# One core, hybrid attention and MLP block: first products a pair of tiles sooner, head mix reordered on GpSimd, a weight combination ahead of the token mixes

## What is computed

```python
h = rmsnorm(x, norm_mix)
proj = h @ w_in                                    # heads of two kinds and 8 gates
mixed = concat(swa_attention(...), forgetting_attention(...))
x = x + mixed @ w_out
h = rmsnorm(x, norm_mlp)
u = relu(h @ w_up)
x = x + (u * u) @ w_down
return rmsnorm(x, norm_final)
```

## Time and profile before

| | |
|---|---|
| median of 3 runs | 2398.11 us (2395.19 to 2401.05) |
| the profiled execution | 2394.05 us, its span 2392.4 us |
| TensorE matmul busy | 97% of the span |
| VectorE, ScalarE, GpSimd busy | 64%, 48%, 30% |
| mean granted clock of TensorE | 0.995 |

### The profile page before, as it was taken

One profiled execution on the slowest core, in us unless ns is written; L12 is line 12 of the kernel. 1 busy time (PEld: TensorE's weight loads), 2 busy tenths in 40 slices (PEclk: granted clock), 3 DMA queues, 4 the chain that ended last, 5 costly groups with the idle time before them and its releaser, 6 DMA issues.

```text
span 2392.4 us, 34959 instructions
## 1 busy us (share of the span) xinstructions
PE 2326.6 (97%) x11346; PEld 1934.7 (81%) x11346; DVE 1520.1 (64%) x2623; ACT 1154.1 (48%) x2226; POOL 706.9 (30%) x593
## 2 busy tenths in 40 slices
PE   7999999999999998999899999999999999999998
PEld 5888888788888886887687877888888888888887
DVE  6588873688888886566745655444465555564454
ACT  5211112788888886223545555555553233333243
POOL 2000000111111114235568764666640032120132
PEclk9999999999999999999999999999999999999999
DMA  5567765666666565766455576654457486564464
GB/s 189 215 235 278 268 242 163 180 160 156 160 157 157 152 156 169 248 218 202 170 183 163 189 286 242 202 160 152 154 190 260 165 298 234 193 219 162 138 219 160
DMA packets 253970, 469.09 MB, mean 196 GB/s; under 512 B 59336, under 2 KB 119752, under 8 KB 246032
## 3 DMA queue, kind: packets, MB, share of 16 engines
q1 hardware_dynamic: 247808, 451.11, 58.6%
q0 software_dynamic: 6048, 16.52, 2.6%
HBM read 316.13 MB, written 151.42 MB: 195 GB/s over the span
## 4 chain that ended last, share of the span: by engine, by line
PE 51%; DVE 3%; POOL 2%; issue 2%; DMA 1%; ACT 1%; SPq 0%; POOLq 0%; ACTq 0%; DVEq 0%
PE m_ps L2533 24%; PE m_ps L2556 23%; PE m_ps L1685 4%; DMA b_kept<-f_kept 1%; POOL m_mix L1548 1%; DVE f_up_lo L2389 1%; PE m_ps L2574 0%; DVE m_xn L1653 0%; DVE m_xm L1646 0%; DVE m_mix L1622 0%; ACT m_mix_hi L1585 0%; DVE keep_lo L2408 0%; POOL h_raw L1560 0%; POOL f_kept L2157 0%; DVE hop_lo L1659 0%
## 5 line engine op out<-in xcount | busy, mean ns | idle before, releaser
L2556 PE MATMUL m_ps<-keep_hi,hop_hi 128*128 128x512 f32 x880 | 342.5, 389 | 0.4 <-DVE hop_lo L2392 0.4
L2556 PE MATMUL m_ps<-keep_hi,hop_lo 128*128 128x512 f32 x880 | 342.4, 389 | 0.0
L2556 PE MATMUL m_ps<-keep_lo,hop_hi 128*128 128x512 f32 x880 | 342.3, 389 | 0.0
L2392 DVE TENSOR_TENSOR hop_lo<-h_raw,hop_hi 128x512 fp32r<-128x512 f32 x224 | 176.6, 789 | 236.8 <-ACT hop_hi L2228 236.7
L2389 DVE TENSOR_TENSOR f_up_lo<-wide_raw,f_up_hi 128x512 fp32r<-128x512 f32 x160 | 182.5, 1142 | 223.0 <-ACT f_up_hi L2223 222.9
L2228 ACT ACTIVATE hop_hi<-h_raw 128x512 fp32r<-128x512 f32 x224 | 140.8, 630 | 334.4 <-PE m_ps L2556 330.5
L958 POOL DMA_DIRECT2D o_main<-a_o x63 | 36.5, 580 | 775.2 <-ACT a_o L1326 726.6
L599 PE MATMUL p_ps_o<-p_ht_lo,p_w_hi 128*128 128x512 f32 x576 | 224.5, 390 | 0.0
L2533 PE MATMUL m_ps<-keep_hi,f_up_hi 128*128 128x512 f32 x512 | 202.8, 396 | 6.1 <-DVE f_up_lo L2389 4.7
L2533 PE MATMUL m_ps<-keep_hi,f_up_lo 128*128 128x512 f32 x512 | 201.3, 393 | 0.0
L2533 PE MATMUL m_ps<-keep_lo,f_up_hi 128*128 128x512 f32 x512 | 199.4, 390 | 0.0
(11 more groups left out here) (246 smaller groups left out, 5779.8 us busy)
## 6 DMA issues: line engine op xcount, KB each, us to landing
h_raw<-u_ops SPq DMA_DIRECT2D x224, 256.0 KB, 4.2
wide_raw<-in_w_up SPq DMA_DIRECT2D x32, 1024.0 KB, 7.2
u_ops<-f_u SPq DMA_DIRECT2D x128, 256.0 KB, 4.3
wide_raw<-in_x SPq DMA_DIRECT2D x59, 512.0 KB, 4.0
u_ops<-f_us SPq DMA_DIRECT2D x96, 256.0 KB, 2.3
proj_hi<-p_o_hi SPq DMA_DIRECT2D x17, 1024.0 KB, 6.2
proj_lo<-p_o_lo SPq DMA_DIRECT2D x17, 1024.0 KB, 8.3
h_raw<-in_w_down SPq DMA_DIRECT2D x58, 256.0 KB, 3.9
```

The lines of the kernel that those rows point to most:

```text
L2392: nc.vector.tensor_tensor(lo, a_raw[:, (m - UP) % A_RING], hi.bitcast(F32), ALU.subtract).then_inc(op_lo_done, 1)
L2556: last = nc.tensor.matmul(down_banks[b % 2][t][:], a[:, cols], w[j], start=(j == 0 and m == 0), stop=(j == FG - 1 and m == 2))
```

## The change

Three edits, told here in the order of the program.

**Start.** Product n stands behind the turn of tile 2n + 3 instead of 2n + 5 (the last two products before stood behind all turns; now only product 7 does). ScalarE's squares of tiles 0 to 3 run up to two tiles ahead, from tile 4 on one ahead as before, and their unused output goes to a part of keep_hi that is written last. The two weight splits stand behind tiles 2 and 3 instead of both behind tile 2; VectorE does norm(4) behind the second; product 0 waits for the first weight split alone. The gate columns are transposed behind tile 5 instead of 7.

**Head mix.** The loops are written so that join, divide and split_mix of tile t + 2 stand at the end of step t. On ScalarE, VectorE and TensorE the resulting order of instructions is what it was. On GpSimd join(t + 2) now waits until norm(t) is done, and mix_tokens stands behind it instead of ahead of it.

**MLP.** GpSimd does mix_w(g + 1, 3) ahead of mix_rest instead of behind it; for g = 15 ahead of the wait and of mix_u too.

```diff
-        GATE_TILE = 7
+        GATE_TILE = 5
-        product_after_turn = {t: 2 * (t // TPB - 1) + t % TPB // 2 for t in range(TPB, ST) if t % 2}
+        product_after_turn = {2 * n + TPB - 1: n for n in range(2 * SB - 1)}
@@ scalar
             square(0)
+            square(1)
             for t in range(ST):
-                if t + 1 < ST:
-                    square(t + 1)
+                for ahead in range(t + 1, min(t + 3, ST)):
+                    if ahead == (t + 2 if ahead < X_RING else t + 1):
+                        square(ahead)
                 if t in product_before_turn:
                     split_first(product_before_turn[t])
                 split_ht_hi(t)
-                if t == 2:
-                    split_w_hi(0)
-                    split_w_hi(1)
+                if t in (2, 3):
+                    split_w_hi(t - 2)
@@ vector
-                if t + 1 < ST:
+                if t + 1 < ST and t != 3:
                     norm(t + 1)
...
-                if t == 2:
-                    split_w_lo(0)
-                    split_w_lo(1)
+                if t in (2, 3):
+                    split_w_lo(t - 2)
+                if t == 3:
+                    norm(t + 1)
@@ tensor
-                pe.wait_ge(w_lo_done, 2)
+                pe.wait_ge(w_lo_done, min(n, 1) + 1)
@@ head mix, gpsimd
+            join(1)
             for t in range(ST):
-                if t + 1 < ST:
-                    join(t + 1)
...
                 nc.gpsimd.tensor_tensor(rstd[:, t:t + 1], rstd[:, t:t + 1], mhalf[:], ALU.pow).then_inc(rooted, 1)
+                if t + 2 < ST:
+                    pool.wait_ge(normed, t + 1)
+                    join(t + 2)
                 if KEPT <= t < KEPT + 6:
                     mix_tokens(t - KEPT)
@@ MLP, gpsimd
             if g == FG - 1:
+                mix_w(g + 1, 3)
                 pool.wait_ge(hop_lo_done, hop_count[1, 1])
             if g:
                 mix_u(g - 1)
+            if g + 1 < GROUPS and g != FG - 1:
+                mix_w(g + 1, 3)
             if 2 <= g < 10:
                 mix_rest(*divmod(g - 2, 2))
-            if g + 1 < GROUPS:
-                mix_w(g + 1, 3)
```

More of the change, by code:

```diff
@@ L232, in project @@
         turned_logits = x_in[:, 0, 0:P]
-        squares = whole.raw["p_o_hi0"][:, S - D:S]
+        squares = whole.raw["keep_hi"][:].rearrange("p (k b) s -> p k (b s)", k=DK // 2)[:, :, S - 2 * P:S]
         gate_first = whole.raw["p_o_lo1"][0:G, S - D:S]
@@ L398, in square @@
                     act.wait_ge(squared, t)
-                nc.scalar.activation(squares, x_in[:, t % X_RING], ACT.Square,
+                nc.scalar.activation(squares, x_in[:, t % X_RING].rearrange("p (k c) -> p k c", k=DK // 2), ACT.Square,
                                      accum_out=ssum[:, t:t + 1]).then_inc(squared, 1)
             def split_ht_hi(t):
+                if t == ST - 2:
+                    act.wait_ge(squared, ST)
                 for half in range(2):
@@ L418, in split_first @@
             def split_first(n):
-                if n == 4:
-                    act.wait_ge(squared, ST)
                 split_o_hi(n % 2, n // 2, n % 4, n)
@@ L445, in _ @@
                 split_ht_hi(t)
-                if t == 2:
-                    split_w_hi(0)
-                    split_w_hi(1)
-            for n in range(2 * SB - 3, 2 * SB - 1):
-                split_first(n)
+                if t in (2, 3):
+                    split_w_hi(t - 2)
+            split_first(2 * SB - 2)
             split_w_hi(2)
@@ L625, in _ @@
                     product_first(product_after_turn[t])
-            for n in range(2 * SB - 2, 2 * SB):
-                product_first(n)
+            product_first(2 * SB - 1)
             def scores_first():
@@ L1599, in _ @@
             act.sem_inc(mix_hi_done, 1)
+            split_mix(1)
             for t in range(ST):
-                if t + 1 < ST:
-                    split_mix(t + 1)
-                else:
+                if t == ST - 1:
                     mlp.scalar_first(act)
@@ L1614, in _ @@
                     nc.scalar.activation(hop_hi[:, k], raw[:, 0, k], ACT.Copy).then_inc(hop_hi_done, 1)
+                if t + 2 < ST:
+                    split_mix(t + 2)
             mlp.scalar(act, lambda: copy_ht(ST - 1))
@@ L1632, in _ @@
             dve.sem_inc(mix_lo_done, 1)
+            divide(1)
+            split_mix(1)
             for t in range(ST):
                 slot = t % 2
[L1635 to L1638, removed]
+                if t == ST - 1:
                     mlp.vector_first(dve)
@@ L1660, in _ @@
                                             ALU.subtract).then_inc(hop_lo_done, 1)
+                if t + 2 < ST:
+                    divide(t + 2)
+                    split_mix(t + 2)
             mlp.vector(dve)
```

## The result

The changed kernel takes 2411.1 us (median of 4 runs, 2409.39 to 2412.16) against 2398.07 for the kernel before in the same session, 13.0 us more. The ratio of the timed runs is 1.0059, 95% interval 1.0047 to 1.0071: 0.6% slower. The forecast was a median near 2410, slower, with a range of 2401 to 2416. The profiled execution has a span of 2409.6 us, 17.2 more than the one of before; the granted clock of TensorE falls from 0.995 to 0.992 in the mean.

A forecast was written before the change was run, and what follows sets the result against it. TensorE, busy 97% of the span, was taken as the bound. Start +10.7, head mix +1.6 and MLP -0.2 gave 12.1 us on 2394.05, so 2406.2; with the median 4.1 above that execution, near 2410, range 2401 to 2416.

The forecast's parts named there:

- The stalls: Start: TensorE waits for the just-turned tile's low half, 4.6 us at products 2 and 4, 2.3 at product 6; sum 11.5.
- the chain of 6.07 us: Start of the kernel before: from product 1's end to the odd tile's second low half done, 6.07 us, carried over unchanged.
- The lead: Start: product 0 runs from about 20.4 to 27.7, a lead of 6.0 us, 4.3 left after two tile turns.
- The clock: Start: lower TensorE clock behind the stalls, 1.5 us for each long one, 0.5 for the short; 3.5 together (0 to 5.5).
- The start in all: Start: lead, stalls and clock summed, -4.3 + 11.5 + 3.5 = 10.7 us lost (6.4 to 13.4).
- Head mix: Tiles 8 to 13: norm runs alone, but mix_tokens beats divide, lengthening the chain 0.3 us a tile (0.1 in tile 8); +1.6.
- Rival 1: Head mix: divide wins against mix_tokens, -3.5 us over five tiles; total 5.1 us less than forecast, 2405; chance 0.12.
- MLP: Group 5's wait goes, -1.4 us; group 16's early mix_w delays splits, +1.2; together -0.2 us (-1.4 to 0).
- Rivals 2 to 4: 2: start stalls shorter, 2402, chance 0.12; 3: no even-product stalls, 2395, 0.07; 4: larger gains, 2385 to 2393, 0.05.

The follow-up runs named there:

- e4_short_chain: Kernel of e1_start with, for odd tiles from 5 on, the next tile's square and norm behind that tile's copies and low halves; ratio 1.0021.
- e1_start: Kernel before with the start's edit alone, head mix and MLP as before; ratio 1.0046.
- e5_high_first: Kernel of e4_short_chain with the start's products running high-half matmuls first, and a product's result split behind the next two tiles' splits; ratio 0.9994.
- e7_order_kept: Kernel before with squares two ahead, second weight split behind tile 4, product 0 waiting for the first split alone, products behind the same tiles; ratio 0.9995.
- e3_divide_first: Kernel of e2_rest with mix_tokens waiting for the same tile's divide, and group 16's early weight combination taken back; ratio 0.9966.
- e2_rest: Changed kernel with the start of before, so head mix and MLP edits alone; ratio 0.9991.

## Why the prediction was right

- **The stalls.** Foretold were 4.6, 4.6 and 2.3 us; from the time at which the product could have started it was 44.62 - 40.0 = 4.6 (its wait shown as 4.38), the same at product 4, and 82.97 to 85.35, 2.4, at product 6. Carrying the chain of 6.07 us over from a place where nobody waited for it was the step that decided the sign. e4_short_chain, where the next tile's square and norm stand behind it, brings 4.4 us down to 2.
- **The lead.** The term was mis-sized: -4.3 with product 0 from 20.4 to 27.7, measured start 20.99 (VectorE's first norm, which waits for a DMA, was 0.47 us later in this execution) and a duration of 8.30 us rather than 7.3. Net of the two turns it was -4.4 + 1.7 = -2.7 us. In e1_start product 0 took 7.28.
- **The clock.** Priced at 3.5 us, measured 8.30 + 7.68 - 2 * 5.56 = 4.9 us; 3.8 in e1_start. It lies within the bounds of 0 to 5.5; the price by product 0 of before was too low, because its five slow matmuls were only the end of a slow stretch. That stretch began with the turn of tile 4 at 22.96 and ended at 29.16. Behind the long waits of the changed kernel no turns stand ahead of the product, which takes the whole stretch: 9 to 13 of its 24 matmuls were slow, not five, at some 0.2 us each.
- **The start in all.** 10.7 us foretold (6.4 to 13.4). At product 6 it was 13.8 in the changed kernel, just above that range, of which 0.5 is the later first norm, and 11.5 in e1_start.
- **Head mix.** +1.6 foretold, +1.5 and +1.4 measured; the other kernels with the head mix of before, e1, e4, e5 and e7, show 0.0 to +0.5, so the change's own share is 1.1 to 1.3 us, as the distances from norm to norm say too. GpSimd did win the race by 0.07 us, in all six tiles that have a mix_tokens, and the norm-to-addition chain grew by 0.26 us. Rival 1, the order that didn't come about, was priced at -3.5 us over five tiles against before; forced in e3_divide_first it brought -4.6. The Trainium skill, "SBUF — State Buffer", section "SBUF: two separate sides", says that whichever starts first has the shared ports for its whole instruction. The traces agree: the second engine's instruction ended only behind the first one's, 1.1 us (divide, norm) or 2.3 us (the join of before) later, which is nearly its whole time alone.
- **MLP.** -1.4 in group 5 and +1.2 in group 16 foretold; the wait of 1.37 us is gone, and the waits of group 16 are 5.7 and 5.8 us in all with the early combination (changed kernel, e2_rest), 4.4 to 4.9 in nine profiles without it, but 5.9 in the tenth (e7_order_kept). The first of them is 3.0 and 3.3 against 1.7 to 2.3 in all ten. So some +1.0, as foretold, on two profiles.

Rivals 2 to 4 fell with the first waits. The sum was 12.1 us; the medians say 13.0. That these agree within 1 us is in part luck: the profiled execution says 17.2, of which 2.2 lie in the attention, and the medians of the two halves run alone, +10.9 (e1_start) and -1.8 (e2_rest), add up to 9.1. What the runs bear out is the stalls, their cause and the sign; the size is known to a few us.

## What to carry to other kernels

Moving a consumer up in the order makes a chain the critical one that was slack before: look up how long it takes where nobody waits, and cut what stands in it for others (the next tile's square and norm) before moving. Split a wait by operand, so that the work on what is ready first goes ahead (the high halves): with both, and the split of the product's result moved back, waits of 4.4 us became 0.3 to 0.5 here. Where GpSimd and VectorE meet, look which of the two is on the chain, and make the other one wait for it: one wait turned a loss of 1.4 us (e2_rest) into a gain of 4.6 (e3_divide_first).

## What the runs showed of the hardware that was not expected

- TensorE's clock fell behind waits of 2 us and less as well, but not each time: behind 1.68 us (e5_high_first, 7.14 us for a product) and 2.06 (e4_short_chain, 7.15), and not behind 2.01, 2.07 or 2.13. Behind 4.37 and 4.38 us it fell in four of four cases, for 1.6 to 2.7 us of extra time.
- GpSimd doesn't win every race. In tile 8 of before, whose norm and mix_tokens stand behind the same root, VectorE began 0.10 us sooner, and GpSimd's instruction was the one that was stretched:

```profile
1051.91 1.28 DVE L1653 SCALAR_TENSOR_TENSOR m_xn<-m_xm,m_rstd,m_gain 128x1024 f32<-128x1024 f32 x1 [2.13 <-POOL m_rstd L1573]
1052.01 3.45 POOL L1560 TENSOR_TENSOR wide_raw<-h_raw 128x1024 f32<-128x1024 f32 x1
```

- A stretch that no edit touches (the attention, 494 us long) moved by up to 4.5 us from one execution to the next, through waits for DMAs. So the span of one profile can't carry an argument of 0.2%. A stage of it carries one only where the waits that changed are read in it: the head mix, for one, differed by 0.0 to 0.5 us from before in the four kernels (e1, e4, e5 and e7) that leave it as it was.
